# Groups of seven products in five column pairs of the early projections

## The reference

```
u = rmsnorm(h, norm_mix_g);  proj = u @ w_in           # 2048 x 7696
qa, ka, va, qb, kb, vb, g_low, ob_gate, gate_a, gate_b = split(proj)
ya = sliding_window_attention(qa, ka, va, ...) @ w_proj_a
ob = rmsnorm(gated_linear_attention(qb, kb, vb, log_a), gla_norm_g)
yb = (ob * silu(ob_gate)) @ w_proj_b
merged = sigmoid(gate_a) * ya + sigmoid(gate_b) * yb
h = h + merged @ w_out                                 # 2048 x 2048
z = rmsnorm(h, norm_ffn_g)
h = h + (silu(z @ w_ffn_gate) * (z @ w_ffn_up)) @ w_ffn_down
```

## Time and profile before

| | us |
|---|---|
| median of 3 runs | 2528.8 (2528.5 to 2529.35) |
| profiled execution, first to last instruction (span) | 2526.1 |
| median of the runs less that span | 2.7 |
| PE busy | 2504.1 (99%) |
| DVE busy | 1874.6 (74%) |
| ACT busy | 1342.5 (53%) |
| POOL busy | 394.0 (16%) |

### The profile page before, as it was taken

How to read it: one execution, slowest core, us unless ns; L and a number is a source line. 1 busy time by engine, 2 the same in 40 slices (tenths; PEclk the granted TensorE clock), 3 DMA queues, 4 the chain that set the end, 5 groups by cost and what they waited for, 6 DMA issues and landing times.

```text
span 2526.1 us, 32950 instructions
## 1 busy us (share of the span) xinstructions
PE 2504.1 (99%) x11871; PEld 2103.8 (83%) x11871; DVE 1874.6 (74%) x2154; ACT 1342.5 (53%) x1801; POOL 394.0 (16%) x295
## 2 busy tenths in 40 slices
PE   9999999999999999999999999999999999999998
PEld 7889888888888888888789988888888888888887
DVE  5556554555799988999966766565669889988985
ACT  5445454444555555555555554455556655665564
POOL 1001100112212300212112301031132101210121
PEclk9999999999999999999999999999999999999999
DMA  7645556575656566565656655465465566556664
GB/s 243 201 145 156 168 168 191 191 238 179 225 192 203 188 207 226 193 201 194 227 182 183 182 148 157 149 217 175 158 220 190 194 209 207 198 199 205 211 213 161
DMA packets 252754, 485.98 MB, mean 192 GB/s; under 512 B 15339, under 2 KB 38844, under 8 KB 251468
## 3 DMA queue, kind: packets, MB, share of 16 engines
q1 hardware_dynamic: 248604, 463.99, 57.5%
q0 software_dynamic: 3696, 20.00, 2.1%
q10 hardware_dynamic: 320, 0.20, 0.0%
HBM read 478.86 MB, written 5.27 MB: 192 GB/s over the span
## 4 chain that ended last, share of the span: by engine, by line
PE 93%; DVE 3%; ACT 1%; issue 1%; DMA 0%; POOL 0%; ACTq 0%; DVEq 0%; POOLq 0%
PE acc L1667 73%; PE acc L1693 6%; PE unit L1693 4%; PE unit L1721 3%; PE psO L1693 2%; PE psS L1693 2%; PE psO L1895 1%; DVE w_lo L2023 1%; PE psS L1787 0%; ACT w_hi L1382 0%; PE psS L1861 0%; PE unit L1787 0%; DVE b_sum_lo L2215 0%; DMA w_raw<-in_w_o_cross 0%; POOL rtmp L1176 0%
## 5 line engine op out<-in xcount | busy, mean ns | idle before, releaser
L2023 DVE TENSOR_TENSOR w_lo<-w_raw,w_hi 128x1024 fp32r<-128x1024 f32 (+6 forms) x570 | 690.6, 1223 | 444.8 <-ACT w_hi L1382 439.6
L1382 ACT ACTIVATE w_hi<-w_raw 128x1024 fp32r<-128x1024 f32 (+6 forms) x570 | 573.3, 1016 | 429.1 <-PE acc L1667 401.2
L1667 PE MATMUL acc<-w_hi,xT_hi 128*128 128x512 f32 (+4 forms) x2020 | 783.1, 388 | 2.3 <-DVE xT_lo L2133 1.8
L1667 PE MATMUL acc<-w_lo,xT_hi 128*128 128x512 f32 (+4 forms) x2020 | 772.0, 382 | 0.0
L1667 PE MATMUL acc<-w_hi,xT_lo 128*128 128x512 f32 (+4 forms) x2020 | 771.4, 382 | 0.0
L1667 PEld LDWEIGHTS acc<-w_hi,xT_hi 128*128 128x128 f32 x2020 | 379.4, 188 | 71.3 <-issue 3.0
L1667 PEld LDWEIGHTS acc<-w_lo,xT_hi 128*128 128x128 f32 x2020 | 379.0, 188 | 70.0
L1667 PEld LDWEIGHTS acc<-w_hi,xT_lo 128*128 128x128 f32 x2020 | 379.6, 188 | 66.1 <-issue 0.5
L2054 DVE TENSOR_TENSOR w_lo<-w_raw,w_hi 128x1024 fp32r<-128x1024 f32 (+1 forms) x204 | 294.7, 1483 | 37.5 <-ACT w_hi L1411 36.3
L1411 ACT ACTIVATE w_hi<-w_raw 128x1024 fp32r<-128x1024 f32 (+1 forms) x204 | 200.1, 1018 | 106.6 <-PE acc L1667 92.4
L1667 PE MATMUL acc<-w_hi,hT_hi 128*128 128x512 f32 x632 | 247.3, 391 | 2.1 <-DVE w_lo L2023 1.4
(11 more groups left out here) (506 smaller groups left out, 3389.0 us busy)
## 6 DMA issues: line engine op xcount, KB each, us to landing
w_raw<-in_w_in SPq DMA_DIRECT2D x168, 512.0 KB, 3.7
w_raw<-in_w_down SPq DMA_DIRECT2D x110, 512.0 KB, 4.3
w_raw<-in_w_up SPq DMA_DIRECT2D x100, 512.0 KB, 4.1
w_raw<-in_w_ffn_down SPq DMA_DIRECT2D x76, 512.0 KB, 4.6
w_raw<-in_w_ffn_gate SPq DMA_DIRECT2D x68, 512.0 KB, 4.4
w_raw<-in_w_ffn_up SPq DMA_DIRECT2D x68, 512.0 KB, 3.8
w_raw<-in_w_out SPq DMA_DIRECT2D x64, 512.0 KB, 4.1
s_raw<-in_w_up SPq DMA_DIRECT2D x28, 512.0 KB, 6.0
```

The costliest lines, as they stand in the source:

```text
L1382: act.activation(w_hi[:, slot, 0:kc, 0:n], w_raw[:, slot, 0:kc, 0:n], ACT.Copy).then_inc(hi_split, 1)
L1667: ins = pe.matmul(ac[t][:, 0:n], a[:, l0 + c, t * P:(t + 1) * P], w[:, slot, c, 0:n], start=start and c == 0 and m == 0, stop=stop and c = ...
L2023: dve.tensor_tensor(w_lo[:, slot, 0:kc, 0:n], w_raw[:, slot, 0:kc, 0:n], w_hi[:, slot, 0:kc, 0:n].bitcast(F32), ALU.subtract).then_inc(lo_ ...
```

## The change

Five pairs of blocks run with groups: queries 512 to 1023 with keys and values (the pair starts at column 512), the two halves of the second gate, and the two halves of w_out. Two sets of buffers (START, EARLY) hold the sums. All groups of these pairs take their weights from the ring. The pairs of queries and gate are evacuated by a new way ("own"): "shared_to" writes the shared sums to the destination (one ACT copy, four DVE adds), DVE adds the accumulators, ACT scales or applies tanh in place. The input sums of the query pair stand behind the turn of x3 and the second squares; their split behind the first block's last tile. The second half of the slots stands one per 1.55 tiles, in the first gate's blocks; ya0 and ya1 share one slot, yb0 and yb1 another. The output pairs add their shared sums to x as the down projections do; u0 and u1 are turned in the second pair's last tiles, u2 and u3 behind the second and third tile of the feed-forward gate.

```diff
+QKV = sevens((3,), ("01S01S01S0011",), home=START, ring=((0, 1, 2),), sums="dve", lhs="xT")
+SIG_B = sevens((3,), ("01S01S01S0011",), home=EARLY, ring=((0, 1, 2),), sums="dve", lhs="xT")
+OUT = sevens((3, 2), ("0011S01S01S01", "01S01S00001111"), home=EARLY, ring=((0, 1, 2), (0, 1)), sums="dve", lhs="xT")
...
+def block_pair(w, k0, kc, c0, needs, turn, plan, group, between={}, to=None):
+
+
+    what, arg = to or ("add", c0)
+    b = [make_block(w, k0, kc, c0 + 512 * j, 512, group["lhs"], 0, what, arg + 512 * j, needs, turn) for j in range(2)]
+    if to:
+        for x in b:
+            x["own"] = True
...
         if q == group["n"] and part < 4:
-            out.append(("shared", c0, part, group))
-            part += 1
+            out.append(("shared_to", b[0], b[1], group) if to else ("shared", c0, part, group))
+            part += 4 if to else 1
         if k[j] == len(plain):
             out.append(("evac", b[j], (0, 1)))
...
-    out, slots, n = [], list(slots), 0
+    out, slots, n, given = [], list(slots), 0, 0
     for s in dense:
         out.append(s)
         if s[0] == "tile":
             n += 1
-            if n % every == 0 and slots:
+            if n >= every * (given + 1) and slots:
                 out += slots.pop(0)
+                given += 1
     for s in slots:
...
@@ -350,9 +375,11 @@
     S += [("warm", 0), ("gain_T",), T("0a", 0), ("lead",), ("warm", 1), T("0a", 1), ("lead",), part(0, 0), part(0, 1)]
     S += [T("0b", 0), T("0b", 1), ("lead",), part(1, 0), T(1, 0), part(1, 1), T(1, 1), ("lead",)]
     S += [part(2, 0), T(2, 0), part(2, 1), T(2, 1), ("lead",), ("lead",)]
-    S += weave(first[3:], [[T(3, 0)] + ssq(1, 0), [T(3, 1)] + ssq(1, 1), ssq(1, 2), ssq(1, 3) + roots(1)], 1)
+    g = group_of(QKV, 0, 0, DC)
+    S += weave(first[3:], [[T(3, 0)] + ssq(1, 0), [T(3, 1)] + ssq(1, 1) + [("h_sums", g, 0)], ssq(1, 2), ssq(1, 3) + roots(1),
+                           [("h_split", g)]], 1)
     S += [("half_rms",)]
-    S += weave(w(512, 512, "qkva", 512), [[], [], [("bias_row",)]], 1) + w(1024, 512, "qkva", 1024)
+    S += block_pair("w_in", 0, DC, 512, (), 0, QKV["plans"][0], g, {1: [("bias_row",)]}, ("qkva", 512))[0]
...
-    slots += [both("ya0"), both("ya1"), both("yb0"), both("yb1")]
-    S += weave(dense, slots, 2)
+    slots += [both("ya0") + both("ya1"), both("yb0") + both("yb1")]
+    g = group_of(SIG_B, 0, 0, DC)
+    turns = [i for i, s in enumerate(dense) if s[0] == "tile"]
+    half = turns[7 * 8]
+    woven = weave(dense[:half], slots[:28], 2) + weave(dense[half:], slots[28:] + [[("h_sums", g, 0)]], 1.55)
+    last = [i for i, s in enumerate(woven) if s[0] == "tile"][-1]
+    S += woven[:last] + [("h_split", g)] + woven[last:]
+    for j in range(2):
+        S += block_pair("w_in", 0, DC, IN1_GB + 1024 * j, (), 0, SIG_B["plans"][0], g, {}, ("sigB", 1024 * j))[0]
+    g = [group_of(OUT, half, 0, DC) for half in range(2)]
...
-                   [[], both(f"merged{j - 1}")] if j else [], 1)
+                   [[("h_sums", g[0], 0)] if j == 3 else [], both(f"merged{j - 1}")] if j else [], 1)
...
-    blocks = [make_block("w_out", 0, DC, 512 * j, 512, "xT", 0, "add", 512 * j, () if j else merged) for j in range(4)]
-    sums_ = into_norm(2, blocks, {(3, 2): 0, (3, 4): 1, (3, 6): 2})
-    S += sums_[:3] + both("merged3") + sums_[3:]
...
+    one, rest = block_pair("w_out", 0, DC, 0, merged, 0, OUT["plans"][0], g[0], {0: [("h_split", g[0])], 3: both("merged3")})
+    two, more = block_pair("w_out", 0, DC, 1024, (), 0, OUT["plans"][1], g[1],
+                           {1: rest + pieces_of_norm(2, 0), 3: pieces_of_norm(2, 1), 8: both("u0"), 10: both("u1")})
+    assert not more
+    S += one + two + pieces_of_norm(2, 2) + pieces_of_norm(2, 3)
...
-    S += out_of_norm(2, make_block(*gate(0, U_NEEDS)))
+    first = make_block(*gate(0, U_NEEDS))
+    S += after_tiles([("tile", first, k) for k in range(8)], {0: roots(2), 1: both("u2"), 2: both("u3")}) + [("evac", first, (0, 1))]
...
                     home = HOME[group["home"]]
                     units_read(pool, at["unit"] - 1 - units)
                     pool.wait_ge(seven_done, at["seven"] + 1)
-                    pool.wait_ge(sums_kept, 32 * at["kept"])
-                    input_sums(hT, group["l0"], group["summed"], home["whole"], home["sum"])
+                    if at["kept"]:
+                        pool.wait_ge(sums_kept, 32 * at["kept"])
+                    input_sums(LHS[group["lhs"]], group["l0"], group["summed"], home["whole"], home["sum"])
...
+                elif s[0] == "shared_to":
+                    act.wait_ge(seven_done, at["seven"] + 1)
+                    act.activation(own_view(s[1], 0), like(s[1], psS[:].rearrange("p i k -> p (i k)")), ACT.Copy).then_inc(p1_copied, 1)
...
+                    if s[1]["own"]:
+                        for t in range(NT):
+                            v = own_view(s[1], t)
+                            if what == "sigB":
+                                block_read(act, at["block"], t)
+                                act.activation(v, v, ACT.Tanh, scale=stat[:, 6 + t:7 + t]).then_inc(sig_b_tanh, 1)
+                            else:
+                                act.wait_ge(own_added, at["owned"] + t + 1)
+                                act.activation(v, v, ACT.Copy, scale=over_rms(s[1]["norm"], t)).then_inc(acc_free[b % 2][t], 1)
...
+                    if s[1]["own"]:
+                        dve.wait_ge(shared_read, at["group"] + 1)
+                        for t in range(NT):
+                            acc_ready(dve, b, t, last)
+                            v = own_view(s[1], t)
+                            dve.tensor_tensor(v, v, like(s[1], ac[t][:]), ALU.add).then_inc(acc_free[b % 2][t] if what == "sigB" else own_added, 1)
...
                         dve.wait_ge(p1_copied, at["group"])
+                        if group["home"] == EARLY and c0 == 0:
+                            dve.wait_ge(x_again_in, 16)
                         dve.tensor_tensor(x_(0, 0), x_(0, 0), to[:, 0], ALU.add)
...
+                elif s[0] == "shared_to":
+
+                    v = lambda b, t: own_view(s[1 + b], t)
+                    p5, p6, p7 = (like(s[1], x) for x in (psO[:].rearrange("p i k -> p (i k)"), bank[0][:], bank[1][:]))
+                    dve.wait_ge(p1_copied, at["group"])
+                    after(dve.tensor_tensor(v(1, 1), v(0, 0), p7, ALU.add))
+                    dve.tensor_tensor(v(0, 1), v(1, 1), p6, ALU.add)
+                    after(dve.tensor_tensor(v(1, 0), v(1, 1), p5, ALU.add))
+                    dve.tensor_tensor(v(1, 1), v(0, 1), p5, ALU.add).then_inc(shared_read, 1)
```

More of the change, by code:

```diff
@@ L81, with sevens @@
 OWN_PLACE = (0, 2)
-NEAR, FAR = "near", "far"
-def sevens(n, plans, home=NEAR, ring=((), ()), sums="pool"):
-    return dict(n=n, plans=plans, home=home, ring=ring, sums=sums)
+NEAR, FAR, START, EARLY = "near", "far", "start", "early"
+def sevens(n, plans, home=NEAR, ring=((), ()), sums="pool", lhs="hT"):
+    return dict(n=n, plans=plans, home=home, ring=ring, sums=sums, lhs=lhs)
 DOWN = sevens((4, 4), ("00101101S01S01S01S01", "0010S101S010S10S1101"), ring=((1, 3), (1, 3)), sums="dve")
@@ L244, in make_block @@
 def make_block(w, k0, kc, c0, n, lhs, l0, evac, arg=0, needs=(), turn=0):
-    return dict(w=w, k0=k0, kc=kc, c0=c0, n=n, lhs=lhs, l0=l0, evac=evac, arg=arg, needs=needs, norm=NORM_OF.get(w), ahead=0, turn=turn)
+    return dict(w=w, k0=k0, kc=kc, c0=c0, n=n, lhs=lhs, l0=l0, evac=evac, arg=arg, needs=needs, norm=NORM_OF.get(w), ahead=0, turn=turn,
+                own=False)
 def tiles_in(b):
@@ L256, in block_steps @@
     return [("tile", b, k) for k in range(tiles_in(b))] + [("evac", b, (0, 1))]
-def block_pair(w, k0, kc, c0, needs, turn, plan, group, between={}):
-    b = [make_block(w, k0, kc, c0 + 512 * j, 512, "hT", 0, "add", c0 + 512 * j, needs, turn) for j in range(2)]
+def block_pair(w, k0, kc, c0, needs, turn, plan, group, between={}, to=None):
[4 more added lines that the diff above has]
+            x["own"] = True
     plain = [k for k in range(kc // CK) if not 1 <= k <= group["n"]]
@@ L338, with group_of, with_sums @@
 U_NEEDS = ("u0", "u1", "u2", "u3")
+def group_of(plan, half, turn, kc):
+    first = (CK + turn) % kc
+    assert first + CK * max(plan["n"]) <= kc
+    return dict(n=plan["n"][half], summed=max(plan["n"]), l0=first, home=plan["home"], ring=plan["ring"][half], sums=plan["sums"],
+                lhs=plan["lhs"], clear=None)
+def with_sums(steps, group, units):
+    first = [i for i, s in enumerate(steps) if s[0] == "summed"][0]
+    i = [n for n, s in enumerate(steps[:first]) if s[0] == "tile"][-1]
+    return [("h_sums", group, units)] + steps[:i] + [("h_split", group)] + steps[i:]
 def schedule():
@@ L362, in schedule @@
         dense += w(IN1_GA + 512 * j, 512, "sigA", 512 * j)
-    for j in range(4):
-        dense += w(IN1_GB + 512 * j, 512, "sigB", 512 * j)
```

(9 more changed lines are left out.)

34 lines of the change are left out of this document (23 added, 11 removed).

## The result

The changed kernel takes 2540.5 us (median of five, 2539.9 to 2541.0) against 2529.0 (2528.5 to 2530.2) for the one before on the same chip: 11.5 us more, ratio 1.0049 (95% interval 1.0038 to 1.0059). The forecast was 2533.1 us, with a range of 2527 to 2540: the side was right, the size was not.

A forecast was written before the change was run, and what follows sets the result against it. TensorE, busy 99% of the span, was taken as the bound. Terms: -9.5 + 5.6 + 2.9 + 1.2 + 4.1 = +4.3 us, span 2526.1 to 2530.4, plus 2.7 to the median: 2533.1 us, range 2527 to 2540.

The forecast's parts named there:

- place 1: Start of the query pair: PE waits for the first block's evacuation behind POOL's input sums, then for DVE; 5.6 us.
- place 4: Second pair of the output projection: first group's second product waits for DVE's read of the shared banks; 4.1 us.
- the first rival: Clock falls in the waits at query start and second output pair; products behind run at half rate, 2.4 us per fall; 0.28.
- up to 2541.1: Upper end, in us, of the clock-falls rival if the clock falls in both waits.
- The first output pair: First pair of the output projection: starts free, input sums ready early and residual reload wanted later than before; nothing.
- DMA out of the sum: All stages: weights land 3.7 us after issue, well ahead of their splits, same bytes moved; no cost counted.
- Place 3: Start of the second gate: first group's fifth product waits for low halves behind the input sums; 1.2 us.
- the groups' 0.68 each: Fourteen groups, each 21 products replacing 24, 4.76 us instead of 5.44; 9.5 us less on PE.
- place 2: Turns of both attention outputs: two names in a row wait for DVE to read the banks, twice; 2.9 us.
- no waits in the cycles between: Cycles of tile, tile, group: PE hides DVE's added work, with 0.7 us to spare; no cost.
- the forecast's own sign: Forecast counts as wrong if waits stand in the cycles between, among other signs.
- The second rival (short sums): POOL's input sums take 8.7 us at query and second gate starts; 2530.2 us, not slower; chance 0.18.

The follow-up runs named there:

- busy_wait: Changed kernel plus 22 unused products of a constant tile between the query pair's first and second tile, filling TensorE's wait; 2539.2 us.
- late_norm: late_first_group with GpSimd's first norm products held until the second output pair's sixth plain tile, shared steps 2 and 3 one tile earlier; 2534.5 us.
- early_sums: Changed kernel with the second gate's input sums put ahead of the two doubled turns of yT instead of behind them; 2543.8 us.
- late_first_group: Changed kernel with two more plain tiles ahead of the second output pair's first group, u0 and u1 turned one tile later; 2538.0 us.
- mended_gain: Against a kernel with plain queries, four single gate turns, sums between them and late_norm's output: norm gain's load ordered later; 2524.2 us.
- late_second_block: Changed kernel with the query pair's second block starting at the fourth tile instead of the second, its groups two tiles later or more; 2536.5 us.

## Why the prediction was wrong

**The failed step is what stands behind the waits of places 1 and 4.** The forecast let PE go on at full clock, with DVE's steps in time, once each wait had ended. It cost place 1 at 5.6 and place 4 at 4.1; they took 7.3 and 6.1. Two things stood there together: the granted clock at 0.50, and DVE's list.

The forecast had the clock at 1.00 and left its fall to the first rival, with 0.28 and 2.4 us a fall. It fell at both, and the products behind took 2.1 and 1.8 us longer. What I held against it was that the clock stood for 3.7 us at the end of the kernel before, and that my waits of 4.4 and 4.1 were "barely longer". That row spoke for the fall as much as against it: it shows 0.50 just behind those 3.7 us. At place 4 the clock even fell after the wait had ended. The section "HAM oscillation" of the Trainium skill's page "TensorE: Matmul & The Clock Gate", which I had named beside the rival, says a wait of this kind sends the engine down; the trace agrees at both places, and the busy wait shows for place 1 that the idle time is the cause.

But the fall is not shown to be what the time went to. At place 1 busy_wait held the clock at 1.00 and gained 0.1 at most. There POOL's sums took 11.1 us, not the 10.4 taken, and DVE's copy of the bias row, which the forecast did not have, held the group's sixth product. At place 4 no run held the clock, and the rows speak against it: the product at 601.09 in the second group waited for the low halves that DVE had ready only at 601.0 (598.68 and 2.36). DVE was on that chain without a pause from 591.0 on, with two splits of 2.3 us beside POOL's products in place of 1.2. Had PE been 1.8 us earlier, it would by these rows have stood there about as much longer. An estimate from the six traces with this wait of 4.1: where the slow stretch was longer (that group 11.5 to 11.8 us, in place of 10.6), the second group ends 0.7 to 1.0 us later; that much the clock cost there. What gave the time of place 4 back was late_norm, with two more tiles ahead of the group and POOL kept away from DVE's sums.

That 2540.5 lies near the "up to 2541.1" of that rival is luck: two falls at its own 2.4 are 2537.9, and 2541.1 needs 4 us a fall, where the group at place 4 lost 1.8 to 2.9 to it in six traces.

**The first output pair, cost nothing, took 1.8.** I followed its input sums and the reload of the residual to who wants them, and found both early; I did not follow how long weight tiles take to land beside that reload. I had put DMA out of the sum on the tile's 3.7 us, a median over another stretch. Issues of weight tiles, with the median from issue to landing: in the kernel before at 532.4 and 535.1, beside the same loads; in the changed kernel at 542.2 and 542.9; and there from 556 to 570.

```profile
w_raw<-in_w_out SPq DMA_DIRECT2D x2, 512.0 KB, 11.6
...
w_raw<-in_w_out SPq DMA_DIRECT2D x2, 512.0 KB, 9.2
...
w_raw<-in_w_out SPq DMA_DIRECT2D x7, 512.0 KB, 4.0
```

So the trace of before held the slow landing; PE did not wait for it there. In the changed kernel a group keeps its ring slots until DVE has summed them (to 542.2), the tiles are asked for only then, and the wait came through to PE.

**Place 3, 1.2, took 2.3.** The chain was the one forecast (sums after the last turned output, splits, weight sums), but it ended a little later: the half split (w_lo) alone held the third product 1.0, and the two low halves held later ones 0.3 each. It was inside its bound of 2.4.

**Right:** the groups' 0.68 each; place 1's wait in kind (eviction forecast for 43.6 to 44.3, and so it came, because the sums began 0.6 us earlier than forecast and took 0.7 longer); place 2; place 4's wait to a tenth of a microsecond; no waits in the cycles between, but for the 1.8 of the first output pair, which by the forecast's own sign speaks against it. The second rival (short sums) fell: DVE worked beside POOL for the first two thirds of them. By the rule of the Trainium skill's page "SBUF — State Buffer", section "Who interferes with whom", I had weighed POOL's sums alone; early_sums and late_first_group show the rule's other side here, DVE's steps 2.4 to 2.8 times as long beside POOL.

With places 1 and 4 as they came the forecast would have been 2536.8; with the output pair 2538.6, with place 3 2539.7, with place 2 2539.5.

## What to carry to other kernels

A saving of 0.7 us a time, fourteen times, is lost by two waits of 4 to 5 us and some 2 us behind each. Price an idle stretch of TensorE as wait plus a fall of the clock, if rows show the clock low after one as long; then ask which engine would hold the products if the clock did not fall, for only the later of the two counts. Put the first group of a pair so late that its chain (sums, splits, shared banks) has ended, even at the price of a plain tile order that looks worse. When a step is moved on GpSimd, look at what VectorE does in those microseconds, and look in the trace whether the step did move: the gain's load stands later in mended_gain's order and is issued at the same moment. And read an effect of 1 or 2 us in 2500 from the starts at the ends of its stage; the medians here do not tell it.

## What the runs showed of the hardware

VectorE's two-input steps beside GpSimd's: 0.69 against 1.67 us (128x512), 1.67 against 4.72 (four of 128x256); GpSimd's four products of the norm took 7.3 and 8.2 us in such stretches, 6.0 in the changed kernel. The granted clock may fall after the engine is at work again (588.0, a microsecond behind the wait), and behind the same wait of 4.10 us the group's products lost 1.8 us in the changed kernel and 2.9 in late_second_block. Weight tiles of 512 KB took 9.2 us to land beside the loads of x and gain, and 4.0 a few us later.
